# Sum of a filter's absolute taps: from a ones-matrix product and a wide reciprocal to a column per channel block, inverted and spread by products with the identity

## The reference, cut to what matters

```python
h = (hdn @ w3).reshape(length, 2, 2, 512)
h = h * exp(-t * deltas)
taps = concatenate([h[:, :, 0], zeros, h[:0:-1, :, 1]], axis=0)
taps = taps / sum(abs(taps), axis=0)        # one sum for each channel
return rfft(taps, n=2 * length, axis=0)
```

## Time and profile before

| | |
|---|---|
| three runs, median | 1946.11 us (1945.92 to 1949.07) |
| the profiled execution, span | 1946.3 us |
| PE busy | 1873.7 us, 11146 matmuls |
| PE weight loads busy | 1525.9 us |
| DVE busy | 1284.9 us |
| ACT busy | 788.5 us |
| POOL busy | 608.5 us |
| HBM read | 245.29 MB |
| mean granted TensorE clock | 0.987 of full speed |

### The profile page before, as it was taken

One profiled execution on the slowest core, in us unless ns is written; L12 is line 12 of the kernel. 1 busy time (PEld: TensorE's weight loads), 2 busy tenths in 40 slices (PEclk: granted clock), 3 DMA queues, 4 the chain that ended last, 5 costly groups with the idle time before them and its releaser, 6 DMA issues.

```text
span 1946.3 us, 32006 instructions
## 1 busy us (share of the span) xinstructions
PE 1873.7 (96%) x11146; PEld 1525.9 (78%) x11146; DVE 1284.9 (66%) x2122; ACT 788.5 (41%) x1627; POOL 608.5 (31%) x553
## 2 busy tenths in 40 slices
PE   6999899999999999999999999999998899999999
PEld 2556788767588888877888887787787789999999
DVE  4754867666856755358765776759686655567574
ACT  2325633356243333333222232356535545445453
POOL 3433243722312111163200223444555521143030
PEclk8999899999999999999999999999999999999999
DMA  6433111232234443344555556233214335554554
GB/s 226 139 107 105 38 56 55 87 121 80 84 130 152 130 161 118 95 134 160 185 173 186 174 194 196 87 87 87 77 44 136 104 109 176 177 168 156 180 183 140
DMA packets 210925, 252.98 MB, mean 130 GB/s; under 512 B 11715, under 2 KB 176900, under 8 KB 209796
## 3 DMA queue, kind: packets, MB, share of 16 engines
q1 hardware_dynamic: 207088, 235.01, 38.2%
q10 hardware_dynamic: 3732, 16.60, 2.3%
HBM read 245.29 MB, written 6.29 MB: 129 GB/s over the span
## 4 chain that ended last, share of the span: by engine, by line
PE 73%; issue 10%; DVE 8%; POOL 5%; ACT 4%; DMA 1%; ACTq 1%; DVEq 0%; POOLq 0%
PE psum L660 58%; PE psum L655 13%; POOL whl L1544 2%; DVE big L2570 2%; PE psum L766 1%; POOL big L3537 1%; ACT whl L1535 1%; ACT big L1783 1%; ACT big L1786 1%; PE psum L628 1%; DVE hhl L2739 1%; DVE big L2579 1%; POOL big L1634 1%; DMA big<-in_hy_table_dram 1%; DVE big L2722 1%
## 5 line engine op out<-in xcount | busy, mean ns | idle before, releaser
L660 PE MATMUL psum<-hhl,whl 128*128 128x512 f32 (+1 forms) x4416 | 826.6, 346 | 11.6 <-DVE hhl L2739 4.3
L660 PEld LDWEIGHTS psum<-hhl,whl 128*128 128x128 f32 x4416 | 693.3, 190 | 132.4 <-issue 24.8
L1535 ACT CAST whl<-raw 128x512 fp32r<-128x512 f32 x656 | 374.1, 618 | 811.6 <-PE psum L660 806.6
L1544 DVE TENSOR_TENSOR whl<-raw,whl 128x512 fp32r<-128x512 f32 x480 | 333.6, 736 | 315.3 <-ACT whl L1535 314.4
L660 PE MATMUL psum<-bigr,whl 128*128 128x512 f32 (+1 forms) x2688 | 474.9, 337 | 1.5 <-DVEq L3314 0.7
L660 PEld LDWEIGHTS psum<-bigr,whl 128*128 128x128 f32 x2688 | 412.8, 190 | 57.2 <-issue 2.2
L1544 POOL TENSOR_TENSOR whl<-raw,whl 128x512 fp32r<-128x512 f32 x176 | 233.6, 1349 | 377.5 <-ACT whl L1535 359.0
L655 PE MATMUL psum<-big 128*128 128x128 f32 (+8 forms) x1572 | 245.7, 326 | 17.9 <-DMA big<-in_hy_w_dram 5.4
L655 PEld LDWEIGHTS psum<-big 128*128 128x128 f32 (+4 forms) x1572 | 164.5, 175 | 77.3 <-issue 51.8
L3537 POOL TENSOR_TENSOR big<-big,tmp 128x512 f32<-128x512 f32 (+1 forms) x64 | 64.5, 1021 | 341.3 <-DVE tmp L3311 340.7
L660 PE MATMUL psum<-whl,hhl 128*128 128x512 f32 x672 | 160.1, 396 | 11.0 <-POOL whl L1544 9.1
(11 more groups left out here) (187 smaller groups left out, 1524.9 us busy)
## 6 DMA issues: line engine op xcount, KB each, us to landing
raw<-in_w_mlp_dram SPq DMA_DIRECT2D x128, 512.0 KB, 3.8
raw<-in_w_in_dram SPq DMA_DIRECT2D x88, 512.0 KB, 3.7
big<-in_w_ada_dram SPq DMA_DIRECT2D x88, 512.0 KB, 5.1
raw<-in_w_gate_dram SPq DMA_DIRECT2D x64, 512.0 KB, 3.5
raw<-in_w_branch_dram SPq DMA_DIRECT2D x32, 512.0 KB, 3.5
raw<-in_w_ada_dram SPq DMA_DIRECT2D x24, 512.0 KB, 5.3
raw<-in_w_o_dram SPq DMA_DIRECT2D x16, 512.0 KB, 3.5
hy_spectra<-big ACTq DMA_DIRECT2D x2, 2560.0 KB, 9.3
```

Of the source, the lines that this page charges most:

```text
L660: m = nc.tensor.matmul(o_, a(p_), b(q_), start=first and i == 0, stop=last and i == 2, skip_group_check=shared)
L1535: nc.scalar.copy(whl[:, r, 0, ks], raw_of(n)[:, ks]).then_inc(S["hi_ready"], 1)
L1544: ins = eng.tensor_tensor(whl[:, r, 1, ks], raw_of(n)[:, ks], whl[:, r, 0, ks].bitcast(F32), ALU.subtract)
```

## The change

The sum over positions is taken with the roles of the two sides exchanged: for each block of 128 channels, the taps are the stationary side and one column of ones is the moving side. The result is one column of 128 sums, channels on partitions, four columns for a filter. The DVE inverts these four columns into `small` and adds to a new semaphore, `hyf_cols`. A new step, `filter_inverse`, spreads them back: PE waits for `hyf_cols`, takes a fill, and multiplies each column (broadcast over 128 columns as the stationary side) with the identity, and the DVE copies this bank to `f_inv[n]`. The new step takes one more of the four work banks. In the diff the parts up to the norm's are PE's, the later ones are the DVE's.

```diff
+        FCOL = 640
...
             def filter_scale(li, n):
                 pe.wait_ge(S["hyf_taps"], 2 * li + n + 1)
                 b = fill(("fs", li, n))
-                for i in range(4):
-                    m = mm(b, ones, f_z1[li][n][:, i, :], i == 0, i == 3)
+                for c_ in range(4):
+                    for i in range(4):
+                        m = mm(b[:, c_:c_ + 1], f_z1[li][n][:, i, c_ * P:(c_ + 1) * P], ones[:, 0:1],
+                               i == 0, i == 3)
+                m.then_inc(filled, 1)
+
+            def filter_inverse(li, n):
+                pe.wait_ge(S["hyf_cols"], 2 * li + n + 1)
+                b = fill(("fi", li, n))
+                for c_ in range(4):
+                    c0 = FCOL + 8 * li + 4 * n + c_
+                    m = mm(b[:, c_ * P:(c_ + 1) * P], small[:, c0:c0 + 1].to_broadcast([P, P]), ident)
                 m.then_inc(filled, 1)
...
                     if g == 4:
                         filter_scale(0, 0)
+                    if g == 5:
+                        filter_inverse(0, 0)
                     if g == 6:
                         filter_spectrum(0, 0)
...
                         if chunk in (8, 16):
                             filter_scale(1, chunk // 16)
+                        if chunk in (9, 17):
+                            filter_inverse(1, chunk // 17)
...
                 norm(li, 0)
                 if li == 0:
+                    filter_inverse(0, 1)
                     filter_spectrum(0, 1)
                 dn(li)
...
             def filter_scale(li, n):
                 b = filled_bank(dve, ("fs", li, n))
-                step(V.reciprocal(f_inv[n], b))
+                c0 = FCOL + 8 * li + 4 * n
+                step(V.reciprocal(small[:, c0:c0 + 4], b[:, 0:4]), S["hyf_cols"])
                 give_fill(dve, ("fs", li, n))
+
+            def filter_inverse(li, n):
+                b = filled_bank(dve, ("fi", li, n))
+                cp(f_inv[n], b)
+                give_fill(dve, ("fi", li, n))
...
                     if g == 5:
+                        filter_inverse(0, 0)
                         filter_spectrum(0, 0)
...
                 dve.wait_ge(S["h_ready"], KD * (nn + 1))
                 if nn == 0:
+                    filter_inverse(0, 1)
                     filter_spectrum(0, 1)
...
                     dve.wait_ge(spectra_kept, 16)
+                    filter_inverse(1, 0)
                     filter_spectrum(1, 0)
...
                     conv_block(8)
+                    filter_inverse(1, 1)
                     filter_spectrum(1, 1)
```

More of the change, by code:

```diff
@@ L401, in build @@
                  "token_copied o_normed stat_ready stat_root q_ready k_ready qkT_ready max_ready "
-                 "exp_ready a_ready aT_ready turns_ready odd_ready eo_ready anti_ready hyk_ready hyf_clear hyf_arg hyf_sin hyf_cut hyf_sums hyf_taps z_ready zf_ready hy_u fn_u fn_v "
+                 "exp_ready a_ready aT_ready turns_ready odd_ready eo_ready anti_ready hyk_ready hyf_clear hyf_arg hyf_sin hyf_cut hyf_sums hyf_cols hyf_taps z_ready zf_ready hy_u fn_u fn_v "
                  "sg_ready mul_done acc_added relu_ready out_ready out_ready_dve out_stored hi_ready lo_ready modrow_ready "
```

## The result

| | before | changed |
|---|---|---|
| median of the runs | 1947.59 us | 1970.31 us |
| profiled execution, span | 1946.3 us | 1968.5 us |
| PE busy | 1873.7 us | 1885.0 us |
| DVE busy | 1284.9 us | 1275.8 us |
| mean granted clock | 0.987 | 0.982 |

The ratio is 1.0121, with a 95% interval of 1.0105 to 1.0137: some 23.6 us slower (20.4 to 26.7) on 1947. I forecast +21.9. The DVE's busy time fell by 9.1 us and the kernel became longer by far more.

A forecast was written before the change was run, and what follows sets the result against it. PE was taken to bound the kernel, busy for 96% of the span. The terms 1.3 + 10.0 + 2.0 + 2.6 + 6.0 gave +21.9 us on 1946.3, about 1968 us, with a range of 1959 to 1977.

The forecast's parts named there:

- (a): Filter (0, 0), ahead of the norm: longer sum and inverse on PE, +1.3 us.
- (e): Clock falls behind the one-column sums of filters (0, 0), (1, 0) and (1, 1): 2.0 us each, +6.0 us.
- (b): Filter (0, 1): PE's fourth spectrum fill waits for a bank the DVE returns only after the norm, +10.0 us.
- (c): After PE's long wait at filter (0, 1), the clock is at 1.2 GHz: +2.0 us.
- (d): Filters (1, 0) and (1, 1): longer sums and inverses where PE is full, twice +1.3, +2.6 us.
- The DVE's gain: Four long reciprocals go: 2.5 us saved on the DVE per filter, 10 us in all, costed at nothing.
- The sign that I had set for (a): POOL's first operation of the norm moves from 69.18 to 70.5, or 73 or so if the clock falls.
- The sum of (0, 1) is hidden: Filter (0, 1)'s longer scale and inverse, 1.3 us more, lie ahead of PE's bank wait and are hidden by it.
- Rival 1: All else holds but the clock does not fall behind narrow products: +15.9 us, 1962; chance 0.28.
- Rival 2: The bank wait at filter (0, 1) does not bind: 1950 to 1956 us; chance 0.07.
- rival 3: The DVE sets the pace and its saving counts: 10 us at most, 1936; chance 0.03.
- rival 4: Clock down longer behind each scale (+4.2), or one-column products cost the upper bound (+7): 1972 to 1980 us; chance 0.12.

The follow-up runs named there:

- experiment 5: Kernel before with its four 128x512 reciprocals replaced by plain copies: ratio 1.0006, again 0.9996; separately, kernel before with fp32r sums: 1940.52 us.
- experiment 3: Changed kernel with the DVE's copy of filter (0, 1)'s inverse moved forward and sums of 128 moving columns: 1948.82 us, ratio 1.0017.
- experiment 4: Kernel before plus one unread fill whose bank the DVE gives back only behind its wait for the norm's eight tiles: 1956.02 us, ratio 1.005.
- experiment 2: Changed kernel with 128 moving columns instead of one in each product of the sums: 1959.64 us, ratio 1.0073.
- experiment 6: Experiment 1 repeated: 1962.14, 1965.33 us; experiment 3 with only filter (0, 1)'s sum one-column: 1953.7 us; kernel before with the change in layer 1 only: 1958.13 us.
- experiment 1: Changed kernel with the DVE's copy of filter (0, 1)'s inverse moved forward between norm tiles 0 and 1: 1962.35 us, ratio 1.0082.

## Why the prediction was right, step by step

The wait, the longer products and the falls of the clock were all seen; the sum, 21.9 us, was 1.7 us short of the measured 23.6, which is inside its interval. The rows of the two traces, before and changed, say where it lies:

| | before | changed | more | forecast |
|---|---|---|---|---|
| first sum to second | 17.11 | 19.72 | 2.6 | 3.3, (a) and (e) |
| second sum to third | 51.20 | 63.57 | 12.4 | 12.0, (b) and (c) |
| sum to spectrum of (1, 0) | 9.01 | 13.30 | 4.3 | 3.3, (d) and (e) |
| from there to the sum of (1, 1) | 30.24 | 30.24 | 0.0 | 0 |
| sum to spectrum of (1, 1) | 9.95 | 14.11 | 4.2 | 3.3, (d) and (e) |

Together 23.4 us, and nothing gives it back: the spectrum of (1, 1) starts 22.1 us later (190.53, 168.41), and the spans differ by 22.2.

- **The DVE's gain is worth nothing.** Right: experiment 5 takes 10 to 11 us off the DVE and the time stays. The one reciprocal ahead of the norm was replaced by idle time before 77.18 (3.68 us).
- **(a) and (d), longer sums and inverses**, 1.3 + 2.6 = 3.9 us: +3.3 by experiment 3. At full clock a sum costs 3.68 us from start to start (49.59 to 53.27), at 0.115 an instruction, where I took 0.12; an inverse 0.81 (142.52 to 143.33), where I took 1.0. The sign that I had set for (a) misleads: POOL's first operation moved to 70.48, as if the clock had not fallen, only because this execution was 1.3 us ahead at its first sum.
- **(b) and (c), the held bank and the clock behind it**, 12.0 us: 9.7 alone (experiment 4), 10.9 between experiments 2 and 3, both with 12.0 inside their intervals. PE waited 10.06 us where I had 11. The price of the clock, (c), was 2.4 us where I took 2.0: the fourth fill and the first 60 matmuls behind the wait took 2.79 + 15.29 us, and at full clock 1.75 + 13.95. From `amp` to the end of the first 60 matmuls there were 27.8 us before (68.83 to 85.46 + 11.20) and 40.5 after (70.13 to 95.32 + 15.29): +12.7 in that pair of traces.
- **(e), the clock behind the narrow sums**, +6.0 us at three places: the kind was right and the size too small. Experiment 2 gives 9.4 us, about 4 to either side, which alone would not exclude 6.0. The traces of the changed kernel and of experiment 2 are closer: with one column the stretches are longer by 1.6 us at (0, 0) (19.72 and 18.14), by 3.2 at (1, 0) (13.30 and 10.09) and by 3.1 at (1, 1) (14.11 and 10.99), 7.9 in all. I took 2.0 us for a fall, near the price of the shortest in the trace of before (1.6). Here the clock was at 0.51 for the whole of the 7 us windows at (1, 0) and (1, 1), and the sum of (1, 0) itself took 4.82 us from start to start (132.88 to 137.70).
- **The sum of (0, 1) is hidden.** Nearly right in the changed kernel, where it costs at most 1.3 us (second sum to third, 63.57 us, against 62.30 in experiment 2), and only there: once the bank is given back early it costs 3.7 us (experiment 6). Taken from the 12 us expected of experiment 1, that leaves 8.3, near the 7.6 measured.
- **Rival 1**, that the clock stays up behind gapless products, fell with experiment 2. **Rival 2** fell with the wait of 10.06 us and experiment 4, **rival 3** with experiment 5. Of rival 4 the first half came about in part: the falls cost more than I took at two of the three places.

## What to carry to other kernels

A step that is taken off one engine's list may need a bank, and a bank from a small ring is only as free as its slowest reader's place in its own order: before adding a fill, look at what stands ahead of the give-back. A sum made by one-column products has few columns and all the weight loads; if it must be so, 128 columns cost the same time here and kept the clock. And a reciprocal that fits into an engine's idle time may cost nothing, as these four of 3.36 us did: look at the idle time around it first. Last, two traces are compared from the first instruction that the change touches: the start of this kernel alone, ahead of any such instruction, put 5.5 us between two executions of one kernel.

## What the runs showed of the hardware that was not expected

- Thirty-two fp32 matmul instructions with weights of their own took 3.75 us with 1 moving column and 3.74 with 128.
- The granted clock went to 1.2 GHz at or behind such a gapless run of one-column products at each of the changed kernel's four sums (19 of 19 over all traces), and at none of the sums of the 128-column kernel (0 of 11).
- Two executions of one kernel (experiments 1 and 6) were 10.7 us apart. In the longer one the clock was down for longer ahead of the first sum, which makes 5.5 us of the difference, and behind the first two sums; the other two sums cost the same in both.
